# Seven steps of the first attention woven into the projection of its values, with the projection's columns in another order

## The reference, cut to what matters

```python
def diff_attention(h, w_qkv, ..., subln_g, w_o, lambda_init, cos, sin):
    qkv = h @ w_qkv                      # 256 x 1024 by 1024 x 3072
    q, k, v = jnp.split(qkv, 3, axis=-1)
    # rope on the first 16 of the 64 columns of each q and k head
    ...
    p = masked_softmax(sc, chunk_mask(blk, s)[None, None, None])
    a = p[:, :, 0] - lam * p[:, :, 1]
    o = jnp.einsum('bhqk,bkhe->bqhe', a, v)
    o = rms_norm(o, subln_g) * (1.0 - lambda_init)
    return o.reshape(b, s, D_MODEL) @ w_o
```

## Time and profile before

| | |
|---|---|
| median of 3 runs | 2675.2 us (2674.29 to 2680.39) |
| the profiled execution | 2677.76 us |
| its span, first to last instruction | 2676.0 us |
| mean granted clock of TensorE | 0.982 |
| TensorE busy | 2536.5 us (95%) |
| VectorE busy | 1970.0 us (74%) |
| ScalarE busy | 1286.9 us (48%) |
| GpSimd busy | 743.2 us (28%) |
| chain of work that ended last | TensorE 87%, VectorE 7%, ScalarE 3% of the span |

### The profile page before, as it was taken

One profiled execution on the slowest core, in us unless ns is written; L12 is line 12 of the kernel. 1 busy time (PEld: TensorE's weight loads), 2 busy tenths in 40 slices (PEclk: granted clock), 3 DMA queues, 4 the chain that ended last, 5 costly groups with the idle time before them and its releaser, 6 DMA issues.

```text
span 2676.0 us, 44260 instructions
## 1 busy us (share of the span) xinstructions
PE 2536.5 (95%) x14322; PEld 2227.4 (83%) x14322; DVE 1970.0 (74%) x3577; ACT 1286.9 (48%) x1913; POOL 743.2 (28%) x754
## 2 busy tenths in 40 slices
PE   7779997899999999999999999889998999999998
PEld 6679876898889888888888888679897888888887
DVE  5768756687657998567777777568997567777776
ACT  4656546555544155544444444563165444444443
POOL 0300003000000100245555555230101255555554
PEclk9999999999999999999999999989999999999999
DMA  6135641456554423666666665424513666666664
GB/s 194 55 118 182 190 146 55 140 181 190 170 165 153 150 70 92 208 190 190 191 190 189 190 192 183 133 79 158 150 60 108 211 188 189 189 190 193 190 190 146
DMA packets 169935, 424.64 MB, mean 159 GB/s; under 512 B 13373, under 2 KB 65981, under 8 KB 169070
## 3 DMA queue, kind: packets, MB, share of 16 engines
q1 hardware_dynamic: 166832, 418.86, 51.0%
q10 hardware_dynamic: 3006, 4.49, 0.5%
HBM read 420.11 MB, written 3.18 MB: 158 GB/s over the span
## 4 chain that ended last, share of the span: by engine, by line
PE 87%; DVE 7%; ACT 3%; issue 2%; POOL 0%; DVEq 0%; DMA 0%; SPq 0%; POOLq 0%; ACTq 0%
PE PS L459 18%; PE PS L460 18%; PE PS L461 18%; PE PS L692 13%; PE PS L774 8%; PE PS L694 7%; PE PS L802 3%; DVE oh L2054 1%; ACT arena L1031 1%; PE PS L641 1%; PE PS L749 1%; DVE lo L1413 1%; DVE xx L1461 1%; DVE oh L2051 0%; PE PS L621 0%
## 5 line engine op out<-in xcount | busy, mean ns | idle before, releaser
L1413 DVE TENSOR_TENSOR lo<-raw,hi 128x1024 fp32r<-128x1024 f32 x716 | 1061.8, 1507 | 513.7 <-ACT hi L931 511.5
L931 ACT ACTIVATE hi<-raw 128x1024 fp32r<-128x1024 f32 x716 | 747.2, 1052 | 325.5 <-PE PS L461 303.2
L459 PE MATMUL PS<-hi,Ah 128*128 128x512 f32 x1024 | 403.1, 394 | 11.2 <-DVE lo L1413 7.1
L460 PE MATMUL PS<-lo,Ah 128*128 128x512 f32 x1024 | 402.5, 393 | 0.0
L461 PE MATMUL PS<-hi,Al 128*128 128x512 f32 x1024 | 399.8, 390 | 0.0
L692 PE MATMUL PS<-xx,hi 128*128 128x512 f32 x1504 | 371.4, 389 | 0.0
L459 PE MATMUL PS<-xx,hi 128*128 128x256 f32 x1152 | 328.7, 285 | 3.2 <-DVE xx L1461 3.2
L692 PEld LDWEIGHTS PS<-xx,hi 128*128 128x128 f32 x1504 | 282.3, 188 | 58.6
L460 PE MATMUL PS<-xx,hi 128*128 128x256 f32 x1152 | 327.6, 284 | 0.0
L461 PE MATMUL PS<-xx,lo 128*128 128x256 f32 x1152 | 327.5, 284 | 0.0
L1334 ACT ACTIVATE gl<-gl 128x256 f32<-128x256 f32 x188 | 78.6, 418 | 481.1 <-DVE gl L2097 481.1
(11 more groups left out here) (241 smaller groups left out, 3566.1 us busy)
## 6 DMA issues: line engine op xcount, KB each, us to landing
raw<-in_peer_u SPq DMA_DIRECT2D x256, 512.0 KB, 3.6
raw<-in_peer_v SPq DMA_DIRECT2D x256, 512.0 KB, 4.4
raw<-in_ffn_w_up SPq DMA_DIRECT2D x88, 512.0 KB, 3.7
raw<-in_ffn_w_down SPq DMA_DIRECT2D x44, 512.0 KB, 4.2
raw<-in_peer_w_q SPq DMA_DIRECT2D x32, 512.0 KB, 4.5
raw<-in_da_w_qkv SPq DMA_DIRECT2D x24, 512.0 KB, 4.1
raw<-in_conv_w_in SPq DMA_DIRECT2D x24, 512.0 KB, 3.9
raw<-in_attn_w_qkv SPq DMA_DIRECT2D x12, 512.0 KB, 4.0
```

The costliest lines, as they stand in the source:

```text
L459: pe.matmul(o, ah, bh, start=start, stop=False)
L460: pe.matmul(o, ah, bl, start=False, stop=False)
L931: cp.activation(hi[:, s, 0:size], raw[:, s, 0:size], ACT.Copy).then_inc(hi_made, 1)
L1413: V.tensor_tensor(lo[:, s, 0:size], raw[:, s, 0:size], hi[:, s, 0:size].bitcast(F32), ALU.subtract).then_inc(lo_made, 1)
```

## The change

The columns are loaded in the order q first half, k first half, q second half, k second half, v, v. A half is heads 0 to 3 or 4 to 7, pairs 0 to 3 or 4 to 7 of the attention. Rope is done by halves of the heads instead of by queries and keys: after groups 0 and 1, during the splits of group 3's blocks, for the first half; during the first two splits of group 5's blocks for the second half. `da_rows_ready` now counts halves, and each pair waits for its own half.

`attention` becomes two functions on TensorE, ScalarE and VectorE, one for a single step and one for the rest. On TensorE steps 0 to 3 stand behind the four blocks of group 4, and steps 4 to 6 behind the first three blocks of group 5. On ScalarE steps 0 to 3 stand each behind one split of group 5's blocks, then the copy of group 4, steps 4 to 6, and the copy of group 5. VectorE has the same order, with the rope of the second half ahead of steps 0 and 1. GpSimd's program is the same. The loop on TensorE is written out, and the DMA of the bias table goes from the start of the attention on ScalarE to a place ahead of the splits of group 5's blocks. The other two attentions call all their steps at once, as before.

```diff
@@ -307,7 +307,7 @@
         da.hb, da.otmp = view(21504, 5, 384), view(24064, TT, P)
-        da.tmp = view(21504, 2, TT, 32, DA_ROT // 2)
+        da.tmp = view(20992, 2, TT, 16, DA_ROT // 2)
@@ -357,6 +357,10 @@
+        def rows_wanted(a, j):
+            return 1 + j // 4 if a is da else 1
         def new_pairs(a, s):
@@ -460,7 +464,7 @@
-            def rows_group(B, G0, per, ncol, k0=0, ex=0):
+            def rows_group(B, G0, per, ncol, k0=0, ex=0, behind=None):
@@ -476,6 +480,8 @@
                     i.then_inc(split_used, 1)
+                    if behind:
+                        behind(b)
                 fresh[0] = None
@@ -591,9 +597,7 @@
                                           ("qT_made", "kT_made", "max_made", "w_made", "pT_made", "values_made"))
-                pe.wait_ge(S(f"{nm}_rows_ready"), 1)
-                for s, v in bank_free[4]:
-                    pe.wait_ge(s, v)
+                rows = S(f"{nm}_rows_ready")
                 count = [0]
@@ -603,6 +607,7 @@
                     b = aux((nm, "qk", j), free, bank())
+                    pe.wait_ge(rows, rows_wanted(a, j))
                     for t in range(TT):
@@ -665,9 +676,16 @@
                         values(s - 7)
-                ao = S(f"{nm}_o_read")
-                acc_free[groups[-1]] = acc_free[groups[-1] - 1] = [(ao, 2 * DA_H if a is da else 5)]
-                bank_free[4] = [(ao, 2 * DA_H if a is da else 5)]
+                def rest(first):
+                    for s in range(first, a.nsub + 7):
+                        step(s)
+                    ao = S(f"{nm}_o_read")
+                    acc_free[groups[-1]] = acc_free[groups[-1] - 1] = [(ao, 2 * DA_H if a is da else 5)]
+                    bank_free[4] = [(ao, 2 * DA_H if a is da else 5)]
+                return step, rest
@@ -833,14 +851,18 @@
                       start=True, stop=True).then_inc(aux_full, 1)
-            with pe.Fori(0, 2, 1) as it:
-                for g in (2, 3):
-                    for s in tcopy:
-                        pe.wait_ge(s, g - 1 + it * 2)
-                    rows_group(B + 4 * g, G0 + g, [2] * 4, 512, 0, it * 8)
+            for g in (2, 3):
+                for s in tcopy:
+                    pe.wait_ge(s, g - 1)
+                rows_group(B + 4 * g, G0 + g, [2] * 4, 512)
+            step, rest = attention(da, (G0 + 6, G0 + 7))
             for g in (4, 5):
+                for s in tcopy:
+                    pe.wait_ge(s, g - 1)
+                rows_group(B + 4 * g, G0 + g, [2] * 4, 512, 0, 0,
+                           lambda b, g=g: step(4 * (g - 4) + b) if g == 4 or b < 3 else None)
                 acc_free[G0 + g] = [(s, g + 1) for s in tcopy]
-            attention(da, (G0 + 6, G0 + 7))
+            rest(7)
             acc_free[G0 + 4] = acc_free[G0 + 5] = [(S("da_o_read"), 2 * DA_H)]
@@ -1043,12 +1065,18 @@
-                if a is gqa:
+                def turn_v():
                     act.wait_ge(aux_full, aux_at[(nm, "v")])
...
                             PS[:, aux_bank[(nm, "v")], :].rearrange("p (t g d) -> p t g d", t=TT, d=GQA_DH)).then_inc(S("v_turned"), 1)
-                cp.activation(small[:, 58:59], ss[:, 4:5], ACT.Exp, scale=0.0)
-                for s in range(a.nsub + (11 if a is da else 6)):
+                def step(s):
+                    if a is gqa and s == 0:
+                        turn_v()
+                    if s == 0:
+                        cp.activation(small[:, 58:59], ss[:, 4:5], ACT.Exp, scale=0.0)
                     for j in new_pairs(a, s) if s < a.nsub else ():
@@ -1073,10 +1101,17 @@
                         cp.activation(sink_e, sink_e, ACT.Square, scale=2.0, bias=minus1).then_inc(S("sink_exp"), 1)
-                splits_to(plan[f"{nm}_wo"][0] + AHEAD)
-                if a is da:
-                    act.wait_ge(S("da_ms_made"), 1)
-                    cp.activation(rst_root, sst, ACT.Sqrt).then_inc(S("da_rt_made"), 1)
+                def rest(first):
+                    for s in range(first, a.nsub + (11 if a is da else 6)):
+                        step(s)
+                    splits_to(plan[f"{nm}_wo"][0] + AHEAD)
+                    if a is da:
+                        act.wait_ge(S("da_ms_made"), 1)
+                        cp.activation(rst_root, sst, ACT.Sqrt).then_inc(S("da_rt_made"), 1)
+                return step, rest
@@ -1106,7 +1141,7 @@
                 else:
-                    cp.activation(qkv[:, 0, bass.ds(g * 512 + ex * 512, 512)], src, ACT.Copy,
+                    cp.activation(qkv[:, 0, bass.ds(g * D + it * 512, 512)], src, ACT.Copy,
                                   scale=rstd[:, 0:1]).then_inc(S("copied_act"), 1)
@@ -1115,14 +1150,18 @@
                     qkv_copy(g, it)
+            act.wait_ge(S("rel_table"), 1)
+            act.dma_start(dtab, dsb[0:GQA_H, :]).then_inc(S("table_out"), 16)
+            step, rest = attention(da)
             for b in range(4):
                 split(B + 20 + b)
+                step(b)
             qkv_copy(4)
+            for s in (4, 5, 6):
+                step(s)
             qkv_copy(5)
             nxt[0] = B + 24
-            act.wait_ge(S("rel_table"), 1)
-            act.dma_start(dtab, dsb[0:GQA_H, :]).then_inc(S("table_out"), 16)
-            attention(da)
+            rest(7)
             act.wait_ge(S("table_out"), 16)
@@ -1711,7 +1762,8 @@
                 else:
-                    V.tensor_scalar(qkv[:, 1, bass.ds(g * 512 + it * 1024, 512)], src, rstd[:, 1:2], None,
+                    c = g % 2 * D + g // 2 * 512
+                    V.tensor_scalar(qkv[:, 1, c:c + 512], src, rstd[:, 1:2], None,
                                     ALU.mult).then_inc(S("copied_dve"), 1)
@@ -1729,30 +1781,41 @@
-            def rope_heads(x, t):
-                dve.wait_ge(S("copied_act"), 2 * x + 2)
-                dve.wait_ge(S("copied_dve"), 2 * x + 2)
-                cos = con[:, C_DCOS + t * R:C_DCOS + (t + 1) * R].unsqueeze(1).to_broadcast([P, 16, R])
-                sin = con[:, C_DSIN + t * R:C_DSIN + (t + 1) * R].unsqueeze(1).to_broadcast([P, 16, R])
-                rope(heads[:, t, x, :, 0:R], heads[:, t, x, :, R:2 * R], cos, sin, da.tmp[:, 0, t, 0:16], da.tmp[:, 1, t, 0:16])
+            def rope_heads(half, t):
+                dve.wait_ge(S("copied_act"), 2 * half + 2)
+                dve.wait_ge(S("copied_dve"), 2 * half + 2)
+                cos = con[:, C_DCOS + t * R:C_DCOS + (t + 1) * R].unsqueeze(1).unsqueeze(1).to_broadcast([P, 2, 8, R])
+                sin = con[:, C_DSIN + t * R:C_DSIN + (t + 1) * R].unsqueeze(1).unsqueeze(1).to_broadcast([P, 2, 8, R])
+                part = heads[:, t, :, 8 * half:8 * half + 8, :]
+                t1, t2 = (da.tmp[:, c, t].rearrange("p (x g) d -> p x g d", x=2) for c in range(2))
+                rope(part[:, :, :, 0:R], part[:, :, :, R:2 * R], cos, sin, t1, t2)
             clear_keys(da)
+            one, rest = attention(da)
             for g in range(5):
...
                     split(B + 4 * (g + 1) + b)
-                    if g in (2, 4) and b % 2:
-                        rope_heads(g // 2 - 1, b // 2)
-                if g == 4:
+                    if g == 2 and b % 2:
+                        rope_heads(0, b // 2)
+                    if g == 4:
+                        if b < 2:
+                            rope_heads(1, b)
+                        if b == 1:
+                            V.tensor_copy(small[:, 5:6], neg_lam).then_inc(S("da_rows_ready"), 1)
+                        one(b)
+                if g == 2:
                     V.tensor_copy(small[:, 5:6], neg_lam).then_inc(S("da_rows_ready"), 1)
...
                                     ALU.mult).then_inc(S("rel_table"), 1)
+            for s in (4, 5, 6):
+                one(s)
             qkv_copy(5)
             nxt[0] = B + 24
-            attention(da)
+            rest(7)
             turned("oda", subg)
@@ -2269,7 +2332,7 @@
-            even("da_qkv", I["da_w_qkv"][0], 6)
+            even("da_qkv", I["da_w_qkv"][0], 6, (0, 2, 1, 3, 4, 5))
             wide("da_wo", I["da_w_o"][0], KD)
```

More of the change, by code:

```diff
@@ L650, in attention @@
                     i.then_inc(aux_full, 1)
-                for s in range(a.nsub + 7):
+                def step(s):
+                    if a is gqa and s == 0:
+                        turn_v()
                     for j in new_pairs(a, s) if s < a.nsub else ():
@@ L887, in _ @@
             acc_free[G0 - 1] = acc_free[G0 - 3]
[L888 removed]
+            attention(mla, (G0, G0 + 1))[1](0)
             acc_free[G0 - 2] = acc_free[G0 - 1] = [(S("mla_o_read"), 5)]
@@ L1244, in _ @@
                 cp.copy(mk[:, 0, 4 * g:4 * g + 4, 0:MLA_NOPE], both[:, :, 0, :]).then_inc(S("copied_act"), 1)
-            attention(mla)
+            attention(mla)[1](0)
             turned("omla", None)
@@ L1639, in head_out, with step @@
                                                da.otmp[:, t, :], ALU.mult, ALU.add).then_inc(S("da_o_read"), 1)
```

(56 more changed lines are left out.)

36 lines of the change are left out of this document (7 added, 29 removed).

## The result

The changed kernel takes 2684.5 us (median of 9 runs, 2683.5 to 2686.3), the kernel before on the same chip 2676.0 (9 runs, 2674.0 to 2680.4): a ratio of 1.0026, with a 95% interval of 1.0017 to 1.0035. That is some 7 us slower by the ratio (4.5 to 9.4 by its interval), 8.5 by the medians. A second measurement of the same kernel later gave 1.0025 (1.0016 to 1.0033). The slowdown is real; by the ratio it is just under the 0.3% that stood as the bound, by the two medians (0.32%) just over it. The profiled execution took 2686.3 with a span of 2684.5, 8.5 more than the profiled execution of before.

What follows compares the result with a forecast made beforehand. TensorE was taken to bound the projection, VectorE the attention. A 7.2 us gain less 8.6 of stalls gave +1.4; clock losses of 2.0 and 1.8 made +5.2, so 2680.4 us, range 2668 to 2686.

Steps and rivals of the forecast that it cites:

- slower: Rival: low clock after the second stall lasts through block 23, costing 7.2 instead of 1.8; +10.6, 2685.8 us; chance 0.16.
- What bounds the stretch: Last projection groups bound by TensorE, attention by VectorE (26.4 of 28 us busy); VectorE reaching step 8 sets attention's end.
- First stall: TensorE idle 5.0 us, from 71.65 to 76.7, at step 0's scores, waiting for pair 0's keys and queries.
- The two engines in turns: VectorE and ScalarE each idle while the other works; splits start at 80.3, 86.8 and 92.6, some 6 us apart.
- Second stall: TensorE idle 3.6 us from 95.08 at full clock, waiting for VectorE's finish 0 before turning step 0's weights.
- The clock: TensorE drops to half clock behind both stalls, losing 2.0 us after the first and 1.8 after the second.
- the sum at full clock: Group 5's end 16.0 us later against 14.6 saved behind it: +1.4 before any clock loss.
- Group 5's end and the keys: Group 5 ends at 105.84 at full clock; from there to pair 5's keys 2.45 us instead of 17.05.
- The parts held at nothing: Four-dimensional rope, moved table DMA and load, column order and straight code taken as 0; rope up to 3.3 us in range.
- No loss from the clock: Rival: the clock holds in TensorE's two stalls; +1.4, 2676.6 us; chance 0.15.
- the weaving works: Rival: VectorE and ScalarE are early enough in the v groups, TensorE alone decides; -7.2, 2668.0 us; chance 0.12.
- Neutral for another reason: Rival: something after step 8 sets the attention's end; within 2 of 2675 us; chance 0.07.

Runs made afterwards that it cites:

- experiment 2: Changed kernel plus idle transposes in TensorE's two stalls (36 ahead of the first wait, 24 ahead of the second): 2680.5 us, ratio 1.0005 to the kernel before.
- Experiment 5: Changed kernel with TensorE's steps one block later, and ScalarE and VectorE copying group 5 ahead of step 6: 2675.9 us, ratio 0.9992 to the kernel before.
- experiment 1: Changed kernel with column order, ropes by halves and straight code kept, but no step woven: 2677.7 us, ratio 0.9998 to the kernel before.
- experiment 8: Changed kernel plus 13 and 9 idle transposes ahead of the two waits of the norm behind the output projection: 2681.2 us, ratio 1.0009 to the kernel before.
- experiment 6: Against the changed kernel, only three steps woven, in group 5, ScalarE and VectorE doing them after all splits: 2672.3 us, ratio 0.9973 to the kernel before.
- experiments 4: Changed kernel with TensorE's scores 0 and steps 1 to 5 one block later, step 6 behind group 5: 2682.9 us, ratio 1.0016 to the kernel before.

## Why the prediction was right, point by point

The mechanism was right: two stalls of TensorE, each with low clock behind it, where they were forecast. The number is less good than that. The measured 2684.5 lies inside the range, but outside the forecast's own band (2678 to 2683), and is nearer to the 2685.8 of the rival "slower".

- *What bounds the stretch.* Right. From the keys of pair 5 on, the attention takes as long as before (+5.66 at the keys, +5.68 at its end), and VectorE's busy share is the same.
- *First stall*: 5.0 forecast, 4.49 measured. It starts at 71.7 as worked out; the queries come 0.5 earlier, since split 20 starts at 70.93 instead of 71.35. Before, ScalarE stood 0.58 behind the end of block 16 (70.77), now 0.26 (70.67); I had kept the old distance.
- *The two engines in turns*: 80.3, 86.8 and 92.6, with 2.0 for the clock 82.3, 88.8 and 94.6; measured 82.37, 88.76 and 94.40. This close fit is in part luck: the queries came 0.5 earlier, and the first low spell cost 0.5 more.
- *Second stall*: 3.6 forecast, 3.04 measured, from 97.45 where 97.1 was worked out.
- *The clock*: a spell of 5.0 at half clock loses 2.5 (2.0 forecast), one of 3.4 loses 1.7 (1.8). By experiment 2 both together are worth 3.75 at the keys (2.9 to 3.1 against the later profiles), where 3.8 was forecast; without them the change stands at +1.9, where the sum at full clock said +1.4. By the rule of the Trainium skill (TensorE: Matmul & The Clock Gate, section "HAM oscillation") the loss is there, and the trace agrees for these two.
- *Group 5's end and the keys*: 105.84 + 3.8 = 109.6 and 112.1 forecast; 109.4 and 112.52 measured. The stretch gives +5.7 for the forecast +5.2. From group 5's end to the keys the sum had 2.45, and it took 3.13: the walk left out ScalarE, whose copy of group 5 stands behind its soft part of step 6, and the values wait 0.61 for it. Experiment 5 puts the copy first, and that wait goes.
- *The parts held at nothing*: right, by experiment 1, within the 0.3 that its keys come later. The six instructions of a rope call take 1.58 in their new form (1.64 before), and ScalarE's 0.3 is not lost.
- *What was missed.* The sum ended at the attention, as if all behind it moved by one amount. The profiled execution lost 2.8 more there than that of before: 0.7 where the output projection restarts and 2.0 in the norm, both at low clock. That the clock is the cause is shown for the norm (experiment 8), and only seen in the profiles for the 0.7. Whether these losses belong to the change is not shown, and for the norm the record speaks against it: the distance is as long with three woven steps, and 1.4 longer than before with none. The measured interval, 4.5 to 9.4 us, holds +5.2 and +5.7 as well as +8.5, so the whole times don't ask for this term. Why the same two waits cost the clock in one execution and not in another is open.
- *The rivals.* "No loss from the clock" fell with the profile, "the weaving works" with it, for this order of the queues. "Slower" stood on the low clock lasting through block 23 (7.2): it lasted 3.4, so that mechanism did not occur; the time came near its side by another one. "Neutral for another reason" fell with the shift at the attention's end.

The order of the queues, not the amount of idle time, was the cause: with six steps in another order the keys come 5.0 earlier than with seven in this one (experiment 5), and a smaller weave, with scores 0 where their keys are ready and no split behind a soft step, gains (experiment 6: -3.8 at the keys). That seven steps could gain in some order is not shown; five brought no more than three.

## What to carry to other kernels

Idle shares only say how much could be woven; whether it can is read by walking each in-order queue, since a woven step that waits for a round trip over other engines holds the blocks behind it. Weave steps where the engines they need have finished their part of the main work (three steps there gained 3.8 us, seven earlier ones lost 5.7), and look at what each copy or split stands behind. Each wait of TensorE of 2.75 us or more in this stretch, where nothing filled it, was paid twice, by its length and by the work behind it at half clock. And a difference behind the changed stretch, read from one profile of each kernel, has to be looked for in other profiles before it is put down to the change.

## What the hardware showed unexpectedly

- A wait need not lower the clock at once: during the second stall it was still 1.00, TensorE restarted at full clock at 100.49, and the low spell began 1.3 us later, at 101.80.
- The length of one wait did not decide it. A wait of 1.76 left the clock at 1.00 (experiments 4 and 5), waits of 2.08 to 4.49 lowered it. But in the attention of the kernel before, waits of 2.02 at 115.51 and 121.49 left it at 1.00, and one of 2.00 at 131.16 had 0.50 behind it. Two waits of 1.65 and 1.23 lowered it in both profiles of the changed kernel, and the same two left it at 1.00 before. The low spells behind the two stalls lasted 5.0 and 3.4 us; in the second profile of the changed kernel the first lasted some 3.45 (0.53 from 77.05 to 80.50), and the keys came 0.7 earlier.
- 60 idle transposes in two stalls brought 3.75 us back at the keys of pair 5; 22 in the norm brought 2.3 there in the changed kernel's profile, and nothing to the median of the kernel before. One kernel's executions differ by up to 9 us (2673 to 2682 for the kernel before), and the runs don't tell which falls of the clock make that spread.
